# A long convolution's transforms by residues mod 4: half the matmuls of the forward transforms and of the first inverse

## The reference, cut to what matters

```python
def long_conv(u, h_pos, h_neg, bias):
    filt_2l = concatenate([h_pos[:1] + h_neg[:1], h_pos[1:], zeros((1, ch)), h_neg[:0:-1]], axis=0)
    y = irfft(rfft(u, n=2 * seq_len, axis=1) * rfft(filt_2l, axis=0)[None], n=2 * seq_len, axis=1)[:, :seq_len]
    return y + bias * u

def mixer(xm, p, state, grid):                 # the Hyena part
    proj = xm @ p['w_in']                      # q, k, v, o, gates and hy_in (3 x 512 columns)
    u = short_conv(hy_in, p['hy_conv_w'], grid)        # 3 taps, in rows of 64 tokens where latent
    parts = split(u, 3, axis=-1)
    filt = hyena_filters(seq_len, p)
    z = parts[-1]
    for n in range(2):
        z = parts[n] * long_conv(z, filt[n, 0], filt[n, 1], p['hy_bias'][n])
    y = concatenate([y_ml, z], axis=-1) @ p['w_out']
```

## Time and profile before

| | us |
|---|---|
| median of 3 runs | 918.48 (917.35 to 919.62) |
| the profiled execution, its own time | 917.74 |
| its span | 915.9 |
| TensorE busy | 827.9 |
| VectorE busy | 409.7 |
| ScalarE busy | 269.1 |
| POOL busy | 107.0 |

### The profile page before, as it was taken

The page is one execution under the profiler, slowest core; times in us unless marked ns, Lnnn a source line. Parts: engine busy times, 40 slices in busy tenths (PEclk is TensorE's granted clock), DMA queues, the critical chain, the costliest instruction groups (busy, mean ns, idle before and its releaser), DMA issues.

```text
span 915.9 us, 17241 instructions
## 1 busy us (share of the span) xinstructions
PE 827.9 (90%) x6857; PEld 449.2 (49%) x6857; DVE 409.7 (45%) x799; ACT 269.1 (29%) x541; POOL 107.0 (12%) x210
## 2 busy tenths in 40 slices
PE   5898999999999999997998999789999999999900
PEld 1242555555355457554664455455555555555500
DVE  5645721121492491555444774833333333333335
ACT  1676411210200100327232332123333333333332
POOL 4000000000001000001001000022222222222140
PEclk9999999999999999999999999799999999999965
DMA  8958303140705302033009203999999999995162
GB/s 258 414 229 321 127 1 115 69 184 1 275 1 171 109 1 92 24 116 115 1 1 340 119 24 132 418 352 412 417 422 416 418 420 415 419 421 195 41 243 113
DMA packets 40202, 191.41 MB, mean 209 GB/s; under 512 B 4416, under 2 KB 4712, under 8 KB 32529
## 3 DMA queue, kind: packets, MB, share of 16 engines
q1 hardware_dynamic: 28426, 152.50, 41.7%
q0 software_dynamic: 9168, 31.61, 10.0%
q10 hardware_dynamic: 2552, 6.50, 2.0%
HBM read 174.14 MB, written 16.44 MB: 208 GB/s over the span
## 4 chain that ended last, share of the span: by engine, by line
PE 81%; DVE 6%; DMA 5%; ACT 4%; issue 1%; SPq 1%; POOL 0%; DVEq 0%; ACTq 0%; POOLq 0%
PE banks L1919 19%; PE banks L1584 15%; PE banks L1930 9%; PE banks L1814 4%; PE banks L1585 4%; PE banks L1824 4%; PE banks L1546 3%; PE banks L1625 3%; PE banks L1720 3%; DMA arena<-in_w_ada 3%; PE banks L1729 2%; PE banks L1478 2%; ACT arena L755 2%; PE banks L1677 2%; PE banks L1658 1%
## 5 line engine op out<-in xcount | busy, mean ns | idle before, releaser
L1919 PE MATMUL banks<-arena 128*32 128x256 f32 x3072 | 175.7, 381 | 1.5 <-DVE arena L1400 1.5
L1584 PE MATMUL banks<-arena 128*128 128x512 f32 x320 | 164.2, 595 | 2.6 <-ACT arena L708 1.6
L1919 PEld LDWEIGHTS banks<-arena 128*32 128x32 f32 x3072 | 95.7, 110 | 64.9 <-issue 2.3
L1585 PEld LDWEIGHTS banks<-arena 128*128 128x128 f32 x320 | 60.8, 190 | 76.5 <-issue 76.5
L1400 DVE STREAM_TRANSPOSE arena<-arena 128x256 f32<-128x256 f32 x49 | 32.2, 656 | 137.3 <-PE banks L1919 134.4
L1930 PE MATMUL banks<-arena 128*32 128x256 f32 x1536 | 91.7, 379 | 1.0 <-DVE arena L1424 1.0
L1930 PEld LDWEIGHTS banks<-arena 128*32 128x32 f32 x1536 | 50.0, 110 | 33.8 <-DVE arena L1424 1.2
L1585 PE MATMUL banks<-arena 128*128 128x128 f32 x320 | 61.5, 274 | 0.0
L1407 DVE COPY arena<-banks 32x256 f32<-32x256 f32 x98 | 41.4, 422 | 40.6 <-PE banks L1930 39.9
L849 ACT ACTIVATE arena<-banks 32x256 f32<-32x256 f32 x98 | 36.6, 374 | 71.5 <-PE banks L1930 70.9
L1584 PEld LDWEIGHTS banks<-arena 128*128 128x128 f32 x320 | 48.5, 192 | 6.1 <-issue 4.9
(11 more groups left out here) (380 smaller groups left out, 1025.2 us busy)
## 6 DMA issues: line engine op xcount, KB each, us to landing
arena<-in_w_gate SPq DMA_DIRECT2D x16, 2048.0 KB, 21.2
arena<-in_w_up SPq DMA_DIRECT2D x16, 2048.0 KB, 26.4
arena<-in_w_down SPq DMA_DIRECT2D x16, 2048.0 KB, 25.8
arena<-in_w_ada SPq DMA_DIRECT2D x12, 2048.0 KB, 13.7
arena<-in_w_in SPq DMA_DIRECT2D x7, 2048.0 KB, 7.9
expert_output<-arena ACTq DMA_DIRECT2D x49, 128.0 KB, 6.3
expert_output<-arena POOLq DMA_DIRECT2D x1, 4096.0 KB, 20.9
arena<-in_w_out SPq DMA_DIRECT2D x2, 2048.0 KB, 7.7
```

The costliest lines, as they stand in the source:

```text
L1584: M(ps[:, b, :], lhs, hT[:, k, CTX:TOK], start=k == 0, stop=k == KD - 1)
L1585: mm = M(ps[:, b + 1, 0:CTX], lhs, hT[:, k, 0:CTX], start=k == 0, stop=k == KD - 1)
L1919: mm = M(ps[q * LANE:(q + 1) * LANE, 2, 0:2 * P].rearrange("p (g f) -> p g f", g=2), xg[:, k, :], gate_up[e % 3][:, :, k, q * P:(q + 1) * ...
```

## The change

Three things are changed.

First, the latent transform. Tokens are sorted by their residue mod 4, in the order 0, 2, 1, 3, and the 256 frequencies as 0 to 127 and then 255 down to 128, so that all four frequencies that belong together stand at the same place of four blocks. `forward` computes, for each residue class and part, one matmul over 128 tokens and the first 128 frequencies: eight latent matmuls in eight groups. ScalarE copies all ten groups; VectorE makes the spectrum from the classes by butterflies (`spectrum_of`), then the products in wider instructions. Before the first inverse a further butterfly separates the classes again, and the inverse needs two matmuls for each tile. The second inverse has the matmuls it had.

Second, the order. The modulation pieces 8 and 9 stand ahead of the first Hyena group, 10 behind group 3, 11 behind group 8. The first transform stands behind group 8, and the groups 9 to 11 behind it; VectorE's short convolutions 9 to 11 are spread among the products. The k transposes stand behind the k projection, ahead of the second inverse.

Third, the final tokens are stored from SyncE.

```diff
-    split = np.concatenate([np.arange(0, LAT, 2), np.arange(1, LAT, 2)])
-    ang = np.pi * ((split[:, None] * (2 * np.arange(LAT // 2)[None, :] + 1)) % (4 * LAT)) / (2 * LAT)
+    split = np.concatenate([np.arange(r, LAT, 4) for r in RESIDUE])
+    freq = np.concatenate([np.arange(P), np.arange(2 * P - 1, P - 1, -1)])
+    ang = np.pi * ((split[:, None] * (2 * freq[None, :] + 1)) % (4 * LAT)) / (2 * LAT)
...
-    chunks = (ada[0:8] + [hyc[2], ada[8], hyc[0], ada[9], hyc[1], ada[10], ada[11]] + qkvo
+    chunks = (ada[0:10] + [hyc[2], hyc[0], ada[10], hyc[1], ada[11]] + qkvo
...
+    CLASS_AT = [(0, 0), (2, 1), (2, 0), (0, 1), (1, 0), (3, 1), (3, 0), (1, 1)]
+    SUM_AT = [(0, 7), (4, 3), (2, 1), (6, 5)]
...
+        for t in range(NT):
+            sp.wait_ge(S["fin_ready"], t + 1)
+            dst = a["out_p"][0] if t == 0 else a["out_s"][0, (t - 1) * P:t * P, :]
+            sp.dma_start(dst, fin[t]).then_inc(S["y_final"], 16)
+        sp.wait_ge(S["y_final"], 16 * NT)
...
+        def butterfly(a, b, done="dve_chain"):
+            link(TT(a, a, b, ALU.add))
+            link(STT(b, b, -2.0, a, ALU.mult, ALU.add), done)
+        def spectrum_of(o):
+            dve.wait_ge(S["fe_read"], 10 * o + 8)
+            butterfly(X[:, 0:4, :], X[:, 4:8, :])
+            butterfly(X[:, 0:2, :], X[:, 2:4, :])
+            butterfly(X[:, 4:8:2, :], X[:, 5:8:2, :])
...
+        def low_products(o):
+            x, t = (v[:, 0:4, :].rearrange("p (m c) w -> p m c w", c=2) for v in (X, prod))
+            link(TT(t, x, pair(o, 0, 0, (2, 2, MW)), ALU.mult))
+            link(TT(x, x, pair(o, 1, 0, (2, 2, MW)), ALU.mult))
+            link(TT(t[:, :, 0, :], t[:, :, 0, :], x[:, :, 1, :], ALU.add))
+            link(TT(t[:, :, 1, :], t[:, :, 1, :], x[:, :, 0, :], ALU.subtract))
+            link(TT(X[:, 0:2, :], prod[:, 0:2, :], prod[:, 2:4, :], ALU.add))
+            link(TT(X[:, 2:4, :], prod[:, 0:2, :], prod[:, 2:4, :], ALU.subtract))
...
+        for n in range(9):
+            short_conv(n)
+        spectrum_of(0)
+        short_conv(9)
+        low_products(0)
+        short_conv(10)
+        high_products(0)
+        short_conv(11)
+        high_sums("dve_chain")
+        butterfly(X[:, 0:4, :], X[:, 4:8, :], "mul_done")
+        context_products(0)
...
-                lo = CTX + t // 2 + t % 2 * 2 * P
-                pe.transpose(ps[:, 5, t * P:(t + 1) * P], u[:, lo:lo + 2 * P - 1:2], ident)
+                pe.transpose(ps[:, 5, t * P:(t + 1) * P], u[:, CTX + RESIDUE[t]:TOK:4], ident)
...
+                if g < 8:
+                    tb, part = CLASS_AT[g]
+                    mm = M(ps[:, b, :], dft_l[:, tb, part, 0:P], z[:, 1 + tb, :], start=True, stop=True)
...
+        ada_turn(2)
+        forward(0)
+        for n in range(9, 12):
+            pe.wait_ge(S["fe_read"], 10)
+            hyena_group(n)
...
+            for n in range(NB):
+                if n < 2:
+                    pe.wait_ge(S["conv_d"], 11 + n)
...
+                pe.wait_ge(S["mul_done"], 1)
+                for part in range(2):
+                    mm = M(ps[:, b, :], idft_l[:, 0, part, t * P:(t + 1) * P], spec_x[:, SUM_AT[t][part], :],
+                           start=part == 0, stop=part == 1)
```

More of the change, by code:

```diff
@@ L692, in untranspose @@
             link(A(dst[:, 0, blk * P:(blk + 1) * P], ps[:, 6, 0:P], ACT.Copy), "tp_read")
-        for n in range(12):
+        for n in range(9):
             taps(n)
-            if 1 <= n <= 8:
+            if n == 8:
+                ada_row(2)
+            if n:
                 untranspose(n - 1)
         def spectra(o):
-            for g in (0, 2, 4, 6, 8, 9):
+            for g in range(10):
                 act.wait_ge(S["fw_done"], 10 * o + g + 1)
@@ L726, in _ @@
         project_qk(1)
+        for t in range(NT):
+            act.wait_ge(S["kt_done"], t + 1)
+            link(A(k_tok[:, t, :], ps[:, 1 + t % 4, :], ACT.Copy), "qk_read")
         act.wait_ge(S["gate_done"], 1)
@@ L995, in _, with short_conv @@
                         ALU.mult, ALU.add), "xt_d")
-        for n in range(12):
+        def short_conv(n):
             part, blk = ((2, 0, 1)[n // 4], n % 4)
@@ L1054, in products @@
             link(TT(xs, p[2], p[3], ALU.subtract), "mul_done")
-        products(0)
+        for n in range(9):
+            short_conv(n)
[8 more added lines that the diff above has]
+        context_products(0)
         ada_columns(1)
@@ L1075, in _ @@
             link(TT(part0[:, tile, :], part0[:, tile, :], ps[:, 5 + t % 2, :], ALU.mult), "iv_read")
-        products(1)
+        spectrum_of(1)
+        low_products(1)
+        high_products(1)
+        high_sums("mul_done")
+        context_products(1)
         for n in range(5):
@@ L1603, in _, with forward @@
             channel_groups(w, n % 4, 1 + 2 * (n % 2), "hy_done")
-            if 1 <= n <= 8:
+        def forward(o):
+            z = part0 if o else part2
+            for g in range(10):
+                if o == 0 and g < 4:
+                    pe.wait_ge(S["conv_d"], 8 + g // 2)
+                if g >= 4:
+                    pe.wait_ge(S["fe_read"], 10 * o + g - 3)
+                b = 1 + (g + 2) % 4
+                if g < 8:
+                    tb, part = CLASS_AT[g]
+                    mm = M(ps[:, b, :], dft_l[:, tb, part, 0:P], z[:, 1 + tb, :], start=True, stop=True)
+                else:
+                    mm = M(ps[:, b, :], dft_c[:, g - 8, :], z[:, 0, :], start=True, stop=True)
+                mm.then_inc(S["fw_done"], 1)
+        ada_piece(8)
+        ada_piece(9)
+        for n in range(9):
+            hyena_group(n)
+            if n == 8:
+                ada_piece(11)
+            if n:
                 to_tokens(n - 1)
@@ L1607, in _ @@
                 ada_turn(1)
[L1608 to L1628, removed]
+            if n == 3:
+                ada_piece(10)
+        ada_turn(2)
+        forward(0)
+        for n in range(9, 12):
+            pe.wait_ge(S["fe_read"], 10)
+            hyena_group(n)
         def inverse_bank(n):
@@ L1654, in _ @@
             if t < LT:
[L1655 to L1659, removed]
+                pe.wait_ge(S["mul_done"], 1)
+                for part in range(2):
+                    mm = M(ps[:, b, :], idft_l[:, 0, part, t * P:(t + 1) * P], spec_x[:, SUM_AT[t][part], :],
+                           start=part == 0, stop=part == 1)
             else:
-                pe.wait_ge(S["mul_done"], 3)
+                pe.wait_ge(S["mul_done"], 2)
                 M(ps[:, b, :], dft_c[:, 2, :], spec_xc[:, 0, :], start=True, stop=False)
@@ L1668, in _ @@
         project_qk(1)
+        pe.wait_ge(S["qk_read"], 2 * NB)
+        for t in range(NT):
+            if t >= 4:
+                pe.wait_ge(S["qk_read"], 2 * NB + t - 3)
+            for h in range(H):
+                mm = pe.transpose(ps[:, 1 + t % 4, h * P:(h + 1) * P], kT[:, h, t * P:(t + 1) * P], ident)
+            mm.then_inc(S["kt_done"], 1)
         for n in range(5):
@@ L1695, in _ @@
         mm.then_inc(S["gate_done"], 1)
[L1697 to L1703, removed]
         pe.wait_ge(S["gate_read"], 1)
```

98 lines of the change are left out of this document (37 added, 61 removed).

## The result

| | before | after |
|---|---|---|
| median of the runs taken together, us | 918.85 (917.35 to 919.62, 4 runs) | 892.44 (890.79 to 893.82, 4 runs) |
| profiled execution, us | 917.74 | 892.52 |
| its span, us | 915.9 | 890.7 |

After to before is 0.9707 (95% interval 0.9686 to 0.9727): 26.4 us less. The range did not hold.

A forecast was written before the change was run, and what follows sets the result against it. TensorE was taken as the bound, busy 90% of the span with 81% of the chain. Terms -20.6 - 0.6 + 2.2 + 0.5 - 0.2 = -18.7 us gave 899.0 profiled, 899.7 as median; range 896.5 to 903.5.

The forecast's parts named there:

- the outputs: Final stores issued by SyncE instead of POOL: -0.2 us, with ends of -2 and +0.7.
- rival (c): At the kernel's end: the end is POOL's, without it 2 us go, 897.9 or a little less; chance 6%.
- Transforms: Both forward transforms and the first inverse: latent matmuls halve, 6.87 us less in each, -20.6 us in all.
- The ring of four banks: In the forward transform: the banks hold the rate of one-matmul groups of 0.86 us, no wait.
- The row of the third modulation part: TensorE's 0.87 us wait for ScalarE's copy of this row falls to 0.3 behind five token transposes: -0.6 us.
- The k transposes: Moved ahead of the second inverse they cover nothing and open two waits of 1.1 us: +2.2 us.
- VectorE's sums: Butterflies and products at both transforms: 0, up to +2 us; tightest margin 1.6 us, ahead of the q projection.
- rival (d): VectorE becomes the bound if reversed and broadcast operands cost much more; at double price +40, 939.7 us; chance 3%.
- Rival (b): A wait in front of the q projection or modulation piece 11, margins used up: 901 to 903 us; chance 8%.
- Step-4 transposes: Transposes to tokens, reading every fourth word instead of every second: +0.5 us, ends no change and +3.5.
- rival (a): Transposes to tokens that read every fourth word run at half rate: 902.7 us; chance 12%.
- Order of the weights: Modulation pieces moved, piece 11's load the near case: 0, up to +3 us if the q load shares the engines.

The follow-up runs named there:

- e1: The kernel before, with only the five stores of the final tokens moved from POOL to SyncE; 911.84 us, ratio 0.9924 to the kernel before.
- e2: The changed kernel with the five final stores back on POOL, which also waits for them; 900.54 us, ratio 0.9801 to the kernel before.
- e9: The changed kernel plus a small memset on POOL that waits for the fourth of five output tiles; 896.28 us, ratio 0.9753 to the kernel before.
- e6: The changed kernel with the k transposes and their ScalarE copies back between gate matmuls and gate fold; 888.59 us, ratio 0.9678 to the kernel before.
- e10: The changed kernel plus a small copy on ScalarE that waits for the fifth output tile; 891.91 us, ratio 0.9696 to the kernel before.
- e8: The changed kernel plus two unused 2048-wide VectorE instructions ahead of convolution 10; 894.52 us, one run.
- e7: The changed kernel with the first transform back behind all twelve Hyena groups, modulation pieces 10 and 11 just ahead of it; 897.05 us, ratio 0.9754.

## Why the prediction was wrong, point by point

The step that failed is the one on the outputs: "-0.2 us; ends -2 (the 7.5 us that follow the last landing belong in part to POOL) and +0.7". It measured -7.1 in e1 by the medians, -8.1 between e2 and the changed kernel, and -7.6 to -7.7 in the traces. The mechanism had been named, also as rival (c), but its size was taken without a row: 2 of the 7.5 us. Nearly all of the 7.5 were POOL's. Once POOL ends 16 us ahead of VectorE they no longer show (e9 has the case between, where 5.9 are left behind VectorE), and what is left behind SyncE's last landing is 0.4 us. No row of the trace before excluded that, so the term's lower end should have been the full 7.5, and with it the range would have reached 892. The store's own path gained 0.3 us by the landings, against the 0.2 taken, though the working itself (2.9 less 2.8) gives only 0.1: that part was near and never the point.

The other steps, in the order of the working:

- Transforms: -20.6 forecast. 6.87 us for eight latent matmuls at L1654 and 6.87 at the inverse, as said. Right. The second transform has 7.10, but before it had 13.97, so it too lost 6.87:

```profile
301.53 13.97 PE banks L1625 x32
```

- The ring of four banks: ScalarE's copies follow one another at 0.86 us with 0.26 idle between; no wait. Right.
- The row of the third modulation part: no wait is listed, but the last transpose starts at 207.95 and takes 0.11, and the turn starts at 208.21, so some 0.15 us are left where 0.3 was expected. Right within 0.2.
- The k transposes: two waits of 1.1, +2.2. Right, and e6 shows the other side of it.
- VectorE's sums at nothing: the margin of 1.6 us was 1.55. Right; rival (d) with its factor of 1.6 is out, since the trace after has 2.29 us for 2048 columns whether plain (L1025) or with a broadcast operand (L1043), and 1.23 for 1024 with or without the reversed order of blocks (L1054 to L1063). Rival (b) is out for both places.
- Step-4 transposes at +0.5: they cost nothing. From the first hyena group to the modulation piece behind group 3, with three of the eight groups turned to tokens between, pass 157.91 - 120.90 = 37.01 us, 37.03 before. The weight load is a shade longer than the 203 ns of the earlier trace rows, and hidden just so:

```profile
L1633 PEld LDWEIGHTS banks<-arena 128*128 128x128 f32 x32 | 4.5, 207 | 0.8 <-issue 0.8
```

  So rival (a) falls. The rule of the Trainium skill in Advanced Engine Details and Errata (SBUF Cachelines), by which one word in a 16-byte line runs at a lower rate, doesn't show here: the load grew by 4 ns and the pace by nothing. The Trainium skill's other passage, in SBUF - State Buffer (Door 1: The DMA port swizzle), gave 0, and the trace agrees.
- Order of the weights at nothing: no transfer is named ahead of piece 11. Right.
- The rest of the kernel: from the value groups to VectorE's last instruction pass 529.7 us, 529.8 before. Right.

So all terms but one held: together 18.5 us were forecast, 18.4 measured by the medians and 19.1 in the traces. And that one, priced at 0.2, brought 7 to 8. It was the smallest of the forecast, and had the profile's widest unexplained interval beside it.

Rival (c) named the right cause with a chance of 6%; its 897.9 was 5.5 us above what came. What stays open is what POOL does in those 7.4 us: no row of any trace has it.

## What to carry to other kernels

An interval at the end of the span that no row explains is a price to be bounded by its full length, from nothing to all, and not by a guessed share. Look which engine has the last word: here the end comes about 7.4 us after POOL's last act, in the three forms tried, and 3 us after VectorE's if POOL has long been done. So in a kernel like this the closing stores are better issued from SyncE, and POOL given nothing that waits for the last result. And before a block is moved away from a place, ask what it covers there: the k transposes were the cover for ScalarE's copies on both sides, and putting them back (e6) gains the 2.2 us that the change gave away.

## What the runs showed of the hardware that was not expected

- POOL's close: 7.3 to 7.55 us from its last act to the span's end in five kernels, with a store and a wait, a store alone, or a memset of 0.10 us. A late end of ScalarE costs nothing (2.8 us from its copy to the end, in e10).
- A wait can cost more than its length. After TensorE's idle 3.09 us in e8 the granted clock was 0.50 for the next 2 us; the wait of 3.3 us in e7 was not followed by this (1.00 in each stretch behind it). What tells the two apart no run here shows, and e8 was run once.
- From 30 to 50 us the changed kernel was granted 0.85 (e9), 0.91 or 1.00 in different runs with the same work there, and with it the first hyena work starts some 2 us later at 0.91 and 4 at 0.85.
